# Sample attention with gathered pages and four column groups in a two-layer decoder step

## The reference

```python
def one_seq(args):
    ql, qr, cn, kn, pages = args
    past_c = cache_ckv[pages].reshape(-1, R)          # 2048 x 256
    past_k = cache_krope[pages].reshape(-1, QK_ROPE)  # 2048 x 64
    s_past = jnp.einsum('thr,lr->htl', ql, past_c) + jnp.einsum('thd,ld->htl', qr, past_k)
    s_new = jnp.einsum('thr,ur->htu', ql, cn) + jnp.einsum('thd,ud->htu', qr, kn)
    s = jnp.concatenate([s_past * SM_SCALE, s_new * SM_SCALE], axis=-1)
    p = jax.nn.softmax(s, axis=-1)
    return p[..., :L] @ past_c + p[..., L:] @ cn      # 8 heads x 256, one new position
```

## Time and profile before

| | |
|---|---|
| median of 3 runs | 2766.09 us (2763.79 to 2766.82) |
| the profiled execution's own time | 2766.44 us |
| its span | 2764.9 us |
| TensorE busy in the span | 2513.7 us (91%) |
| VectorE, ScalarE busy | 1114.6, 709.9 us |
| mean granted clock of TensorE | 0.953 of 2.4 GHz |
| moved by DMA | 294.53 MB, mean 107 GB/s |

### The profile page before, as it was taken

One profiled execution on the slowest core, in us unless ns is written; L12 is line 12 of the kernel. 1 busy time (PEld: TensorE's weight loads), 2 busy tenths in 40 slices (PEclk: granted clock), 3 DMA queues, 4 the chain that ended last, 5 costly groups with the idle time before them and its releaser, 6 DMA issues.

```text
span 2764.9 us, 47021 instructions
## 1 busy us (share of the span) xinstructions
PE 2513.7 (91%) x19722; PEld 2279.6 (82%) x19722; DVE 1114.6 (40%) x1854; ACT 709.9 (26%) x893; POOL 38.0 (1%) x64
## 2 busy tenths in 40 slices
PE   3999999899995989999969999987889989999997
PEld 2999998888894889999959999986653338999997
DVE  2433234445458443323363333354542223533333
ACT  2322122422222132212251212133342231311212
POOL 1000000000000000000000000000000000000000
PEclk7999999899997899999989999999999999999999
DMA  6453443333332244345315533211123322222321
GB/s 242 143 162 109 146 141 109 123 110 121 119 112 70 63 130 159 122 134 160 91 60 163 165 109 98 72 58 29 54 85 89 89 72 77 74 83 88 105 66 59
DMA packets 351094, 294.53 MB, mean 107 GB/s; under 512 B 35557, under 2 KB 326460, under 8 KB 350944
## 3 DMA queue, kind: packets, MB, share of 16 engines
q1 hardware_dynamic: 346016, 277.14, 32.8%
q0 software_dynamic: 4928, 15.30, 1.5%
HBM read 284.87 MB, written 7.51 MB: 106 GB/s over the span
## 4 chain that ended last, share of the span: by engine, by line
PE 84%; DVE 7%; ACT 3%; DMA 2%; issue 2%; SPq 1%; POOL 0%; DVEq 0%; ACTq 0%; POOLq 0%
PE ps L633 23%; PE ps L635 22%; PE ps L634 22%; PE ps L661 2%; PE ps L1182 2%; PE ps L875 2%; PE ps L1141 2%; DMA raw<-in_hg_w_in 1%; PE ps L1142 1%; ACT w_hi L1249 1%; DVE rstd L1690 1%; DVE rstd L1884 1%; PE ps L1115 1%; PE ps L1096 1%; PE ps L911 1%
## 5 line engine op out<-in xcount | busy, mean ns | idle before, releaser
L633 PE MATMUL ps<-hn_hi,w_hi 128*128 128x260 f32 x3680 | 1069.1, 291 | 53.9 <-DVE hn_lo L1706 47.1
L635 PE MATMUL ps<-hn_hi,w_lo 128*128 128x260 f32 x3680 | 1052.5, 286 | 0.0
L634 PE MATMUL ps<-hn_lo,w_hi 128*128 128x260 f32 x3680 | 1051.8, 286 | 0.0
L633 PEld LDWEIGHTS ps<-hn_hi,w_hi 128*128 128x128 f32 x3680 | 707.3, 192 | 79.7 <-issue 72.3
L634 PEld LDWEIGHTS ps<-hn_lo,w_hi 128*128 128x128 f32 x3680 | 707.0, 192 | 0.0
L635 PEld LDWEIGHTS ps<-hn_hi,w_lo 128*128 128x128 f32 x3680 | 706.9, 192 | 0.0
L1634 DVE TENSOR_TENSOR w_lo<-raw,w_hi 128x2048 fp32r<-128x2048 f32 (+5 forms) x200 | 381.4, 1908 | 436.1 <-ACT w_hi L1249 435.9
L1249 ACT ACTIVATE w_hi<-raw 128x2048 fp32r<-128x2048 f32 (+4 forms) x193 | 319.8, 1657 | 766.3 <-DMA raw<-in_w_ffn_gu 509.4
L633 PE MATMUL ps<-hid_hi,w_hi 128*128 128x260 f32 x1408 | 398.5, 283 | 0.0
L634 PE MATMUL ps<-hid_lo,w_hi 128*128 128x260 f32 x1408 | 398.2, 283 | 0.0
L635 PE MATMUL ps<-hid_hi,w_lo 128*128 128x260 f32 x1408 | 397.3, 282 | 0.0
(11 more groups left out here) (285 smaller groups left out, 2035.5 us busy)
## 6 DMA issues: line engine op xcount, KB each, us to landing
raw<-in_w_ffn_gu SPq DMA_DIRECT2D x176, 512.0 KB
raw<-in_w_ada SPq DMA_DIRECT2D x144, 512.0 KB
raw<-in_w_ffn_down SPq DMA_DIRECT2D x96, 384.0 KB
raw<-in_hg_w_in SPq DMA_DIRECT2D x32, 512.0 KB
pg<-in_cache_ckv SPq DMA_DIRECT2D x128, 128.0 KB, 2.0
raw<-in_w_ffn_down SPq DMA_DIRECT2D x32, 256.0 KB
raw<-in_kv_w_ada SPq DMA_DIRECT2D x16, 512.0 KB
ss<-in_state_hgrn POOLq DMA_DIRECT2D x8, 512.0 KB, 7.6
```

Of the source, the lines that this page charges most:

```text
L633: pe.matmul(out[:, t, :], wh, xh[:, c], start=start, stop=False)
L634: pe.matmul(out[:, t, :], wh, xl[:, c], start=False, stop=False)
L635: mm = pe.matmul(out[:, t, :], wl, xh[:, c], start=False, stop=stop)
```

## The change

- The page table is loaded in eight transfers, so that each of 128 partitions holds the page number of its run of 16 positions (partition 8 n + s: page n, run s). VectorE makes run numbers `idx` from them at the start.
- A sequence's pages come in two indirect transfers issued by GpSimd: one of 128 runs of 16 KB, one of 128 runs of 4 KB. SyncE issues none.
- A partition now holds 16 positions, one in each of 16 column blocks. `turn(b, g)` transposes four blocks of 256 (8 transposes) and two pairs of rotary blocks (2 transposes). Four turns feed four groups g. Their transposed pages have a place each in `cts` and `ctr`; evictions alternate between ScalarE and VectorE.
- `scores(b)` runs once for a sequence: four steps for each of four column groups. Group g writes rows 32 g to 32 g + 31 of one PSUM bank; the queries stand in 32 columns, of which 8 are not zero. The exponential is taken over 128 x 512 straight from PSUM, with the maximum of each row (head and group), its sum is kept for each row.
- `values(b)` is made in four column groups too, copied out unscaled.
- The scores of the new positions of all sequences are made at the start of the stage. Behind the last sequence the groups' maxima and sums are joined, and one series of multiplies combines groups, sequences and new positions.
- The loops are written out. VectorE's order is that of ScalarE; its `queries(b + 1)` and `maxima(b)` stand where ScalarE has `weights(b)`, and it ends a sequence with `values(b)`.

```diff
+RUN = 16
+SUB = PAGE // RUN
...
+        (pg0, pg1, cts), e10 = group(
+            ar, ("pg0", [P, RUN * KV], F32), ("pg1", [P, RUN * KV], F32), ("cts", [P, 4, RK, 512], F32))
+        (srow, pts, ctr, ol_hi, ol_lo, qpad), e11 = group(
+            scr, ("srow", [P, 512], F32), ("pts", [P, 4, P], F32), ("ctr", [P, 4, 256], F32),
+            ("ol_hi", [P, RK, NS, H], F32R), ("ol_lo", [P, RK, NS, H], F32R), ("qpad", [P, 2, 4, GW], F32))
+        (pgk0,), e13 = group(max(e9, e11), ("pgk0", [P, RUN * ROPE], F32))
+        (pgk1,), e14 = group(tabs, ("pgk1", [P, RUN * ROPE], F32))
...
-            def pages(seq, q):
-                sp.wait_ge(pages_used, T.at("seq", 1))
-                for p in range(NPG):
-                    v = sp.value_load(pt_sb[0:1, bass.ds(seq * NPG + p, 1)], min_val=0, max_val=top)
-                    sp.dma_start(pg[q][:, p, :], ckv_pages[:, bass.ds(v, 1), :].rearrange("p a r -> p (a r)")
-                                 ).then_inc(pages_in[q][2 * p // NPG], 16)
-                    sp.dma_start(pgk[q][:, p, :], kr_pages[:, bass.ds(v, 1), :].rearrange("p a r -> p (a r)")
-                                 ).then_inc(pages_in[q][2 * p // NPG], 16)
-                T.add("seq")
...
-            pages(0, 0)
             columns(uv_v, 0, D, 0, RK)
-            columns(ao_v, 0, 256)
-            columns(ao_v, 256, 256)
-            sp.wait_ge(o_read, H)
-            with T.loop(sp, NS // 2 - 1, {"seq": 2}) as i:
-                pages(i * 2 + 1, 1)
-                pages(i * 2 + 2, 0)
-            pages(NS - 1, 1)
-            columns(ao_v, 512, 256)
-            columns(ao_v, 768, 256)
+            for m in range(4):
+                columns(ao_v, m * 256, 256)
...
-            pool.dma_start(pt_sb[:], a["page_table"].rearrange("b n -> (b n)").rearrange("(a n) -> a n", a=1)
-                           ).then_inc(s_pt, 16)
+            for r in range(SUB):
+                pool.dma_start(pt_sb[r:P:SUB, :], a["page_table"].rearrange("b n -> n b"),
+                               allow_slow_non_contiguous=True).then_inc(s_pt, 16)
+            pool.iota(lane[:], [[0, 1]], base=0, channel_multiplier=1).then_inc(lane_done, 1)
...
+            latent_runs = a["cache_ckv"].rearrange("n (s i) r -> (n s) (i r)", i=RUN)
+            rope_runs = a["cache_krope"].rearrange("n (s i) r -> (n s) (i r)", i=RUN)
+            def pages(b):
+                q = b % 2
+                if b >= 2:
+                    pool.wait_ge(pages_used, b - 1)
+                pool.indirect_dma_start(pg[q][:], None, latent_runs, bass.IndirectOffsetOnAxis(ap=idx[:, b:b + 1], axis=0)
+                                        ).then_inc(pages_in[q][0], 16)
+                pool.indirect_dma_start(pgk[q][:], None, rope_runs, bass.IndirectOffsetOnAxis(ap=idx[:, b:b + 1], axis=0)
+                                        ).then_inc(pages_in[q][1], 16)
+            pool.wait_ge(idx_ready, 1)
+            pool.wait_ge(lat_done, 2)
+            pages(0)
+            pool.wait_ge(o_read, H)
+            for b in range(1, NS):
+                pages(b)
...
+            pe.wait_ge(qd_ready, 1)
+            pe.matmul(ps[:, 3, 0:NS * H], dup[:], qrs[:].rearrange("p b h -> p (b h)"), start=True, stop=True
+                      ).then_inc(qd_made, 1)
+            for b in range(NS):
+                o = ps[0:H, 7, b:b + 1]
+                for r in range(RK):
+                    pe.matmul(o, ql[:, r, b, :], cnew[:, r, b:b + 1], start=(r == 0), stop=False)
+                mm = pe.matmul(o, qrs[:, b, :], kr2[0:ROPE, NP + b:NP + b + 1], start=False, stop=True)
+            mm.then_inc(new_mul, 1)
...
+            def turn(b, g):
+                q, n, bank = b % 2, 4 * b + g, 4 * (g % 2)
+                if g == 0:
+                    pe.wait_ge(pages_in[q][0], 16 * (b // 2 + 1))
+                    pe.wait_ge(pages_in[q][1], 16 * (b // 2 + 1))
+                if n >= 2:
+                    pe.wait_ge(ct_copied_a, n - 1)
+                    pe.wait_ge(ct_copied_d, n - 1)
                 for p in range(4):
                     for r in range(RK):
-                        pe.transpose(ps[:, b + r, p * P:(p + 1) * P], pg[q][:, 4 * g + p, r * P:(r + 1) * P], ident)
-                    mm = pe.transpose(ps[0:ROPE, b + 2, p * P:(p + 1) * P], pgk[q][:, 4 * g + p, :], ident)
+                        c = (4 * g + p) * KV + r * P
+                        pe.transpose(ps[:, bank + r, p * P:(p + 1) * P], pg[q][:, c:c + P], ident)
+                for p in range(2):
+                    c = (4 * g + 2 * p) * ROPE
+                    mm = pe.transpose(ps[:, bank + 2, p * P:(p + 1) * P], pgk[q][:, c:c + P], ident)
                 mm.then_inc(ct_t, 1)
...
+            def scores(b):
+                pe.wait_ge(qs_ready, b + 1)
+                pe.wait_ge(ct_copied_a, 4 * b + 4)
+                pe.wait_ge(ct_copied_d, 4 * b + 4)
+                if b:
+                    pe.wait_ge(exp_done, b)
+                for step in range(4):
+                    for g in range(CG):
+                        rows_g = slice(g * GW, (g + 1) * GW)
+                        if step < RK:
+                            o, k = ps[rows_g, 3, :], cts[:, g, step, :]
+                        else:
+                            o = ps[rows_g, 3, :].rearrange("p (a e n) -> p a e n", a=2, e=2)[:, :, step - RK, :]
+                            k = ctr[:, g, :].rearrange("p (a n) -> p a n", a=2)
+                        mm = pe.matmul(o, qpad[:, b % 2, step, :], k, start=(step == 0), stop=(step == 3),
+                                       tile_position=(0, g * GW))
+                mm.then_inc(sc_mul, 1)
+            def weigh(b):
+                pe.wait_ge(exp_done, b + 1)
+                if b:
+                    pe.wait_ge(ol_done, b)
+                else:
+                    pe.wait_ge(sel_ready, 1)
+                for c in range(4):
+                    mm = pe.transpose(ps[:, 7, c * P:(c + 1) * P], srow[:, c * P:(c + 1) * P], ident)
+                mm.then_inc(pts_t, 1)
+            def values(b):
+                pe.wait_ge(pts_copied, b + 1)
+                for c in range(4):
+                    for g in range(CG):
+                        p = 4 * g + c
+                        mm = pe.matmul(ps[g * GW:(g + 1) * GW, 7, 0:KV], pts[:, c, g * GW:(g + 1) * GW],
+                                       pg[b % 2][:, p * KV:(p + 1) * KV], start=(c == 0), stop=(c == 3),
+                                       tile_position=(0, g * GW))
+                mm.then_inc(pages_used, 1)
+            turn(0, 0)
+            turn(0, 1)
+            for b in range(NS):
+                turn(b, 2)
+                turn(b, 3)
+                scores(b)
+                if b + 1 < NS:
+                    turn(b + 1, 0)
+                    turn(b + 1, 1)
+                weigh(b)
+                values(b)
+            pe.transpose(ps[0:NS, 3, 0:P], smx[:], ident)
+            pe.transpose(ps[0:NS, 3, P:2 * P], ssum[:], ident)
+            pe.transpose(ps[0:NS, 3, 2 * P:2 * P + GW], snew[:], ident[0:GW, 0:GW]).then_inc(part_t, 1)
+            pe.wait_ge(wts_made, 1)
+            pe.transpose(ps[:, 2, 0:NS], den[:].rearrange("s g h -> s (g h)"), ident[0:NS, 0:NS]).then_inc(wts_t, 1)
+            pe.wait_ge(selw_done, 1)
+            pe.wait_ge(ol_done, NS)
+            for r in range(RK):
+                rp = slice(r * P, (r + 1) * P)
+                pe.matmul(ps[:, 6, r * 64:(r + 1) * 64], ckn[:, rp], wnz[:].rearrange("s b h -> s (b h)"),
+                          start=True, stop=False)
+                for b in range(NS):
+                    mm = pe.matmul(ps[:, 6, r * 64 + b * H:r * 64 + (b + 1) * H], ol_all[:, b, rp], selw[:, b, :],
+                                   start=False, stop=(b == NS - 1))
+            mm.then_inc(olt_done, 1)
...
+            def copy_pages(b, g):
+                bank = 4 * (g % 2)
+                act.wait_ge(ct_t, 4 * b + g + 1)
+                if g % 2 == 0:
+                    act.activation(cts[:, g, :, :], ps[:, bank:bank + 2, :], ACT.Copy).then_inc(ct_copied_a, 1)
+                else:
+                    act.activation(ctr[:, g, :], ps[:, bank + 2, 0:256], ACT.Copy).then_inc(ct_copied_a, 1)
+            def weights(b):
+                act.wait_ge(smax_done, b + 1)
+                act.activation(srow[:], ps[:, 3, :], ACT.Exp, bias=snb[:, b:b + 1], scale=SM_SCALE,
+                               accum_out=ssum[:, b:b + 1]).then_inc(exp_done, 1)
+            def weights_t(b):
+                act.wait_ge(pts_t, b + 1)
+                act.activation(pts[:].rearrange("p c n -> p (c n)"), ps[:, 7, :], ACT.Copy).then_inc(pts_copied, 1)
+            copy_pages(0, 0)
+            copy_pages(0, 1)
+            for b in range(NS):
+                copy_pages(b, 2)
+                copy_pages(b, 3)
+                weights(b)
+                if b + 1 < NS:
+                    copy_pages(b + 1, 0)
+                    copy_pages(b + 1, 1)
```

(68 more changed lines are left out.)

214 lines of the change are left out of this document (44 added, 170 removed).

## The result

The changed kernel takes 2688.69 us (median of 4 runs, 2684.31 to 2689.33), the kernel before 2765.44 (4 runs, 2763.79 to 2766.82): ratio 0.9719, 95% interval 0.9704 to 0.9735. The forecast was 2683, 5.7 us under that median.

What follows compares the result with a forecast made beforehand. TensorE's column-poor multiplies and SyncE's transfer issue were taken to bound the sample attention. Its 240.2 us become 154.3 (19.4 + six periods of 18.95 + 11.9 + 9.3), plus 3 at the start: gain 83, forecast 2683 us, range 2640 to 2738.

Steps and rivals of the forecast that it cites:

- The two bounds: Old sample attention: TensorE's column-poor multiplies and SyncE's issue of 32 transfers both bound a sequence at 28 to 30 us.
- Column groups: Sample attention: multiplies in four column groups take 2.8 us for scores instead of 11.1, 2.0 for values instead of 7.07.
- Rival 4: Column groups run one after another: scores 10.8 us, values 7.0, period 25.0, gain 21, time 2746 us; chance 0.03.
- A to F: TensorE's cycle: A turns 2 and 3, B eviction, C scores, D next sequence's first turns, E weights, F values; 12.1 us.
- L: Time of one sequence's page gather, 2.62 MB: 10.5 us; the period is the larger of A+B+C and L, plus D+E+F.
- The clock: TensorE's clock falls after each wait of 4.0 us for a gather: 2.9 us lost in each of 6 periods, period 18.95.
- rival 2: TensorE stays at 1.2 GHz throughout the stage: period 21.75 us, gain 41, time 2725 us; chance 0.14.
- The ends of the stage: Sample attention outside the six periods: first values 19.4 us in, last sequence 11.9 us, join 9.3 us.
- The start: Kernel start: VectorE waits for the page table before copying x; copies begin at 25.3 us, 3 us lost.
- 3: Rival: gather at about 160 GB/s, L 18 us, period 26.45, gain 38, time 2728 us; chance 0.10.
- 5: Rival: gather served as small pieces, slower than before; at 69 GB/s L 38 us, period 43.6, time 2831 us; chance 0.04.
- 1: Rival: gather near the engines' peak, L 8.7 us, clock holds, period 14.25, gain 111, time 2655 us; chance 0.17.

Runs made afterwards that it cites:

- k1: Kernel before with GpSimd's two gathers per sequence in place of SyncE's 32 page transfers, multiplies and order unchanged: 2774.45 us, ratio 1.0027 to the kernel before.
- k2: Changed kernel with the old page transfers (SyncE, 32 per sequence) and the old start: 2759.09 us, ratio 0.9976 to the kernel before.
- k12: Kernel before with gathers in place of SyncE's transfers, index steps behind VectorE's copies of x: 2766.68 us, ratio 1.0003 to the kernel before.
- k4b: Changed kernel with a third latent buffer, earlier rotary gather, and the stage's first weight split moved behind the join: 2653.31 us, ratio 0.9581 to the kernel before.
- k3: Changed kernel with weights and values of a sequence ahead of the next one's first two turns: 2676.81 us, ratio 0.9677 to the kernel before.
- k11: Changed kernel without the rotary gather, and TensorE's wait for it, from the third sequence on: 2669.23 us, ratio 0.9656 to the kernel before.
- k5: Changed kernel with VectorE's page table wait and index steps moved behind the copies of x: 2679.14 us, ratio 0.9687 to the kernel before.
- k9: Changed kernel with third latent buffer, moved weight split and index steps behind the copies of x: 2647.30 us, ratio 0.9574 to the kernel before.
- k13: Kernel before, unedited, profiled a second time: 2766.07 us (1 run), stage 240.3 us, 477.9 us behind the split.
- k7: Changed kernel with unread multiplies in TensorE's waits, behind each sequence's scores and in the join: 2674.25 us, ratio 0.9671 to the kernel before.
- k10: Changed kernel with third buffer, moved split, late index steps, and unread multiplies in last sequence and join: 2644.62 us, ratio 0.9565 to the kernel before.

## Why the prediction was right, and where its steps were off

**The two bounds**: right, shown by k1, k2 and k12 together with the changed kernel.

**Column groups**: scores were put at 2.8 and take 2.78 (2075.49 to 2078.27), values 2.0 against 1.93. Rival 4 is out.

**The cycle**: waits A to F were put at 12.1; k4b shows 12.05. That D to F must follow the landed gather is shown by k3 and k4b.

**L** was put at 10.5, it is 10.0 and 9.6 (2090.21 to 2099.82), mean 9.8. The engines move 426 and 410 GB/s in the two stretches shown, above the 405 of the earlier trace rows, and 388 on the mean from 2074.5 to 2080.5. The Trainium skill (DMA: Bandwidth & Descriptors, section Anatomy of one DMA) has nearly that rate, 436 GB/s, but its fixed 2.0 us are too few here: 2.62 MB at 418 GB/s (the mean of the two stretches) are 6.3 us, and 10.0 less 6.3 is 3.7; k11's first, 2.10 MB alone, gives 8.76 less 5.0, again 3.7. By the page L was 8.0; the measurement decides.

**The clock** was charged 2.9 us in each period. The clean one is 15.34 (forecast 16.05), the longest 18.28. From the end of the first values (2071.68) to that of the seventh (2173.51) six periods take 101.8, mean 17.0, not 18.95. From TensorE's start behind the gather to the end of the values (`D` to `F`) the clean period takes 5.4 us and the others 8.0, 7.0, 7.1, 6.8 and 7.0: the clock costs 2.5, 0, 1.6, 1.7, 1.4 and 1.6 us, mean 1.5. The step "2.9 for each of the 6" is the one that failed in size, by 1.4 us a period; the shorter L, 0.7 us, gives the rest. The 2.9 was the loss of 16 transposes and 32 value instructions of the old code, 8.19 us at full clock, and was carried over to 5.55 us of other work. A wait of 3.66 was followed by half clock, one of 3.27 by full clock, but one of 3.13 by half clock again, so the length of the wait alone does not set it. The Trainium skill (TensorE: Matmul & The Clock Gate, section HAM oscillation — how this bites in real kernels) has every step start slow in a kernel whose compute per step is shorter than its wait for data. That condition is not met here, with 12.1 us from `A` to `F` to waits of 3.1 to 3.8, so it gave no ground for rival 2; five of the six periods start at half clock all the same (1.85 us or more for eight transposes that take 1.06), and the clock is back before their values.

**The ends of the stage** were too cheap: first values 22.7 us in (19.4), since TensorE began at 2051.5 and ran the first turns at half clock; last sequence 13.4 (11.9), its values at half clock, 3.58; join 12.8 (9.3), its 32 full-weight instructions 0.22 each instead of 0.11. 22.7 + 101.8 + 13.4 + 12.8 = 150.7, against 154.3: 8.3 us too little at the ends, 11.9 too much in the periods. That these nearly cancel is luck.

**The start** was put at +3 (copies at 25.3). They start at 27.80, because the last of eight loads landed at 27.2, not 24.5, and the first norm is 6.8 later. The late index gives back 8.8 us (k5), 6.6 (k12 against k1) and 1.9 (k9 against k4b) by the ratios; each of these is uncertain by some 4 to 9 us, and the first norm, 4.9 to 6.7 us earlier in the three pairs, is the surer measure.

**Not forecast**: -4.8 and +5.0 us in code that the change leaves alone. The total was nearer than its terms: a stage gain of 85.9 and +3 (82.9) stand against 89.6 and +6.8 -4.8 +0.3 +5.0 = +7.3 (82.3). Against the medians the gain is 76.8, so the agreement to a microsecond is that of one execution.

**The rivals**: L excludes 3 and 5, the falls of the clock exclude 1 as written (it needed L = 8.7 and a clock that holds; k11, with a mean of 8.5, comes near both), and a mean clock of 0.86 excludes 2.

## What to carry to other kernels

Where two resources bound a stage at equal height, removing one shows nothing; judge the pair, and look for the next bound in the order of buffer use rather than in busy shares: here a third buffer, with a weight split moved out of its way, was worth 1.4% on top. Put an index computation's wait where its engine has nothing else to start. Charge the clock for waits as a range and not per wait, and include the short serial ends of a stage.

## What was not expected of the hardware

TensorE's clock also falls while it is fully busy with multiplies of 8 columns behind full weights, and where it does depends on more than the code. Five microseconds from the split on, and the next five: before, then gathers alone with late index, whose instructions there are the same.

```profile
2286.95:2291.95 5.00, 4.39 (x33) 4.39 (x34) 0.52 (x2) 0.00 (x0) 0.00 (x0) 0.85 0.00 0
2291.95:2296.95 5.00, 4.42 (x20) 4.33 (x21) 1.50 (x4) 0.00 (x0) 0.00 (x0) 0.50 0.09 14
```

```profile
2281.53:2286.53 5.00, 4.39 (x21) 4.40 (x21) 0.52 (x2) 0.00 (x0) 0.00 (x0) 0.54 0.00 0
2286.53:2291.53 5.00, 5.00 (x25) 5.00 (x25) 0.00 (x0) 0.00 (x0) 0.00 (x0) 0.50 0.00 0
```

The same busy time at first, 33 instructions against 21. The 48 head products end 2.6 us later behind the split, and 80 instructions in it is 3.1; this is most of the 4.5 us, the rest comes later. Of the 4.8 us ahead of the first state store, 4.3 lie in one stretch, equally far from the first norm; before, then after:

```profile
491.09:541.09 50.00, 44.63 (x365) 41.95 (x365) 21.35 (x34) 16.30 (x20) 0.00 (x0) 0.89 0.40 127
```

```profile
497.92:547.92 50.00, 44.62 (x409) 41.23 (x409) 24.17 (x42) 18.89 (x26) 0.00 (x0) 1.00 0.41 133
```

k13's profile repeats that of before in both places (0.89 there, 0.85 behind the split), k5 and k12 show the other outcome in both, k2 and k4b that of before in this stretch (0.89) and a lower clock behind the split; four kernels lie between (k1, k7, k9 and k10, 0.95 to 0.96). Every other kernel was profiled once. So for the kernel before it isn't chance of a single execution; kernels with gathers show either outcome in the first place, and k2, without them, the slower one in the second. What sets it stays open. It also bounds what can be read from a few microseconds: runs of the kernel before in one job were 2761.95 us at a mean clock of 0.956 and 2772.87 at 0.949.
